# Merge and router of a mixer-and-experts block as one stage, bias parts made in the first stage, tokens turned ahead of the norm

## The reference, cut to what matters

```python
# merge_branches
ya = (rms_norm(from_heads(o_a), gdn_norm_g) * silu(za)) @ w_out_a
yb = (rms_norm(from_heads(o_b), gla_norm_g) * silu(rb)) @ w_out_b
gates = sigmoid(parts[11])
y = (gates[..., :D_MODEL] * ya + gates[..., D_MODEL:] * yb) @ w_out
# first_block
x = x + g1 * y
h = rms_norm(x, norm_ffn_g) * (1.0 + sc2) + sh2
x = x + g2 * moe_ffn(h, ...)
# moe_ffn
logits = h @ w_router + b_router
top_logit, top_idx = lax.top_k(logits, TOP_K)
top_p = softmax(top_logit)
gu = xb @ w_gu[e] + b_gu[e]
glu, lin = minimum(gu[:, :D_EXPERT], 7.0), clip(gu[:, D_EXPERT:], -7.0, 7.0)
act = glu * sigmoid(1.702 * glu) * (lin + 1.0)
y = (act @ w_down[e] + b_down[e]) * p
```

## Time and profile before

| | us |
|---|---|
| median of 3 runs | 2254.32 |
| lowest and highest run | 2253.1, 2254.37 |
| the profiled execution | 2256.12 |
| its span, first to last instruction | 2254.3 |
| TensorE busy | 1987.3 |
| VectorE busy | 699.3 |
| ScalarE busy | 498.1 |
| GpSimd busy | 74.1 |

### The profile page before, as it was taken

One profiled execution on the slowest core, in us unless ns is written; L12 is line 12 of the kernel. 1 busy time (PEld: TensorE's weight loads), 2 busy tenths in 40 slices (PEclk: granted clock), 3 DMA queues, 4 the chain that ended last, 5 costly groups with the idle time before them and its releaser, 6 DMA issues. The chain is left out here.

```text
span 2254.3 us, 25572 instructions
## 1 busy us (share of the span) xinstructions
PE 1987.3 (88%) x9450; PEld 1091.9 (48%) x9452; DVE 699.3 (31%) x1516; ACT 498.1 (22%) x931; POOL 74.1 (3%) x67
## 2 busy tenths in 40 slices
PE   6999796989898469999999999999999697879997
PEld 3346455968786233333333333333333245547774
DVE  1475363447201522221222122212222303332323
ACT  2221721453301011111111111111111203410111
POOL 0000500100000300000000000000000000000000
PEclk8999997989999679999999999999999899889998
DMA  9452346134632469999999999999999334024342
GB/s 330 148 205 90 130 108 137 53 119 129 218 134 85 163 257 417 417 417 418 417 417 418 418 418 417 417 417 418 417 418 418 121 119 162 1 89 165 140 167 84
DMA packets 149817, 565.51 MB, mean 251 GB/s; under 512 B 35840, under 2 KB 43008, under 8 KB 111904
## 3 DMA queue, kind: packets, MB, share of 16 engines
q1 hardware_dynamic: 149760, 564.73, 64.7%
HBM read 554.67 MB, written 10.03 MB: 250 GB/s over the span
## 5 line engine op out<-in xcount | busy, mean ns | idle before, releaser
L1996 PE MATMUL expert_gb<-expert_ring,hT 128*64 128x512 f32 x1024 | 262.6, 592 | 0.0
L1996 PE MATMUL expert_lb<-expert_ring,hT 128*64 128x512 f32 x1024 | 262.5, 592 | 0.0
L2028 PE MATMUL expert_yb<-expert_ring,hT 128*64 128x512 f32 x1024 | 226.8, 595 | 11.2 <-ACT hT L1951 11.2
L1904 DVE TENSOR_SCALAR hT<-expert_gb 128x512 f32<-128x512 f32 x32 | 22.1, 692 | 551.3 <-PE expert_lb L1996 551.3
L1966 PE MATMUL expert_ob<-hT,ob 128*128 128x512 f32 x256 | 125.6, 618 | 36.8 <-DVE oa L1917 24.5
L2608 PE MATMUL ffn_pu<-ffn_hT,ffn_wu 128*128 128x256 f32 x704 | 155.7, 380 | 0.0
L2608 PEld LDWEIGHTS ffn_pu<-ffn_hT,ffn_wu 128*128 128x128 f32 x704 | 134.1, 191 | 27.2 <-issue 9.6
L440 PE MATMUL mix_in_pj<-hT,mix_in_pj_ring 128*128 128x512 f32 (+1 forms) x384 | 144.3, 535 | 1.4 <-DVE hT L551 1.4
L1996 PEld LDWEIGHTS expert_lb<-expert_ring,hT 128*64 128x64 f32 x1024 | 72.3, 137 | 147.5 <-issue 147.5
L2028 PEld LDWEIGHTS expert_yb<-expert_ring,hT 128*64 128x64 f32 x1024 | 70.6, 137 | 148.7 <-issue 128.0
L1917 DVE TENSOR_TENSOR oa<-oa,expert_ob 128x512 f32<-128x512 f32 x128 | 86.4, 685 | 174.6 <-PE expert_ob L1966 174.6
(11 more groups left out here) (466 smaller groups left out, 2398.4 us busy)
## 6 DMA issues: line engine op xcount, KB each, us to landing
expert_ring<-in_w_gu SPq DMA_DIRECT2D x256, 1024.0 KB, 11.9
expert_ring<-in_w_down SPq DMA_DIRECT2D x128, 1024.0 KB, 10.1
fill_w<-in_w_fill SPq DMA_DIRECT2D x48, 512.0 KB, 3.6
mix_in_wm<-in_w_mod SPq DMA_DIRECT2D x11, 2048.0 KB, 9.6
ffn_wu<-in_w_up_units SPq DMA_DIRECT2D x22, 1024.0 KB, 5.9
mix_in_pj_ring<-in_w_in_units SPq DMA_DIRECT2D x12, 1024.0 KB, 4.8
ffn_wd<-in_w_down SPq DMA_DIRECT2D x22, 512.0 KB, 3.4
attend_in_wi<-in_w_in SPq DMA_DIRECT2D x4, 2048.0 KB, 10.8
```

The lines of the kernel that those rows point to most:

```text
L1904: v.tensor_scalar(glu, gb[:], LIMIT, None, ALU.min).then_inc(s_glu, 1)
L1996: m = pe.matmul(b[halves[h], :], xT[:, k, x], ring[:, z, c0 + 512 * h:c0 + 512 * h + 512], start=False, stop=(k == GU - 1))
L2028: m = pe.matmul(yb[halves[h], :], hidT[:, c, hh * SLOTS:(hh + 1) * SLOTS], ring[:, z, a * F + 512 * h:a * F + 512 * h + 512], start=False, ...
```

## The change

- `merge_stage` and `router_stage` become one stage, `merge_route_stage`, without the barrier between them. The stage's large tiles (`pz`, the two branch weights) lie in the expert ring; SP loads the ring's units as these tiles come free: 8 to 11 after the second branch product, 0 to 3 after `y`, 4 to 7 after the last product with `w_out`.
- The bias parts are made in `mix_in_stage` by GpSimd from biases laid out over 128 partitions (768 columns each), stored to DRAM at the end of that stage, and loaded as `bparts` in the merge.
- `x` is transposed before the norm. The router weights are multiplied by `a2`; a row of `b2` times the router weights (the shift, eight matmuls ahead of the later fill units) is added to the router bias; the logits are multiplied by the root of each token. `h2T` is copied by VectorE and ScalarE, in halves. The table of the square root and that of exp are loaded ahead. `xn`, which the experts gather, is made after the mask.
- The one-hot comparisons of all ranks and halves become one operation of 256 elements and a sum; the weights are a product with it and a second sum.
- The memsets of `wgt`, `mask`, `pos`, `posp`, `put` and `acc` are made by GpSimd in the merge.

```diff
@@ mix_in_stage, sync, after gate_cols
+                sp.dma_start(bias[:], A.bias_blocks).then_inc(s_bi, 16)
                 later(4)
@@ mix_in_stage, sync, end
-                sp.wait_ge(s_o, 96)
+                sp.wait_ge(s_bs, 7)
+                sp.dma_start(A.bias_split.rearrange("n p c -> p n c"), parts[:]).then_inc(s_o, 16)
+                sp.wait_ge(s_o, 112)
@@ mix_in_stage
+            @block.gpsimd
+            def _(g):
+                link = Chain(g, s_bs)
+                g.wait_ge(s_bi, 16)
+                for n in range(3):
+                    link(g.tensor_copy(parts[:, n, :], bias[:]))
+                    if n < 2:
+                        link(g.tensor_copy(back[:], parts[:, n, :]))
+                        link(g.tensor_tensor(bias[:], bias[:], back[:], ALU.subtract))
@@ merge_route_stage, sync, after the load of x
+                sp.dma_start(wr, A.w_router.rearrange("(k p) n -> p k n", p=P)).then_inc(s_rw, 16)
...
+                for n in range(3):
+                    sp.dma_start(S.bparts[n * NE:(n + 1) * NE].rearrange("e (b c) -> e b c", b=4),
+                                 A.bias_split[n].rearrange("(b e) c -> e b c", b=4)).then_inc(s_tab, 16)
                 for f in range(F0 + 8, F1):
                     S.fill.load(sp, f)
                 sp.wait_ge(s_pa, 1)
...
+                sp.wait_ge(S.fill.done, F1)
+                sp.dma_start(S.pick, A.bias_pick).then_inc(s_tab, 16)
+                sp.wait_ge(s_pa, 2)
+                for n in range(8, 12):
+                    load_expert_unit(sp, A, S, 0, n)
+                sp.wait_ge(s_y, 1)
+                for n in range(4):
+                    load_expert_unit(sp, A, S, 0, n)
+                sp.wait_ge(s_t, 4)
+                for n in range(4, 8):
+                    load_expert_unit(sp, A, S, 0, n)
+                sp.wait_ge(s_tab, 128)
@@ gpsimd
                 g.tensor_tensor(sq[:], S.oa[:], S.oa[:], ALU.mult).then_inc(s_sq, 1)
+                for b in (S.wgt, S.mask, S.pos, S.posp):
+                    g.memset(b[:], 0.0).then_inc(s_m, 1)
+                g.wait_ge(s_pa, 2)
+                g.memset(S.put[:], 0.0)
+                g.memset(S.acc, 0.0)
@@ scalar
+                act.activation(warm[:], C.eps[:], ACT.Sqrt)
                 for t in range(2):
                     act.wait_ge(s_z, t + 1)
-                    act.activation(junk[:], S.x[:, t, :], ACT.Square, accum_out=ss[:, t:t + 1]).then_inc(s_xs, 1)
-                    act.wait_ge(s_xs, t + 1)
-                act.wait_ge(s_n, 2)
-                act.activation(rstd[:], ss[:], ACT.Sqrt).then_inc(s_n, 1)
+                    act.activation(junk, S.x[:, t, :], ACT.Square, accum_out=ss[:, t:t + 1]).then_inc(s_xs, 1)
+                    act.wait_ge(s_n, 2 * t + 2)
+                    act.activation(rstd[:, t:t + 1], ss[:, t:t + 1], ACT.Sqrt).then_inc(s_rs, 1)
+                for t in range(2):
+                    act.wait_ge(s_tr, t + 1)
+                    act.activation(S.h2T[:, 4:8, t * P:(t + 1) * P], bank[5 + 2 * t][:].rearrange("p a n -> p (a n)")
+                                   .rearrange("p (k n) -> p k n", k=4), ACT.Copy).then_inc(s_xta, 1)
+                act.activation(warm[:], C.eps[:], ACT.Exp)
@@ tensor, before the second branch product
+                        pe.wait_ge(s_rt, 2)
+                        pe.wait_ge(s_wa, 1)
+                        for k in range(KT):
+                            m = pe.matmul(shift, C.ones, wrb[:, k, :], start=(k == 0), stop=(k == KT - 1))
+                        m.then_inc(s_rb, 1)
                         for f in range(F0 + 6, F1):
                             fill(f)
                         pe.wait_ge(S.fill.copied, F1)
+                        pe.wait_ge(s_br, 1)
@@ tensor, after the products with w_out
                 for t in range(2):
-                    pe.wait_ge(s_h, 1 + t)
+                    pe.wait_ge(s_z, 1 + t)
                     for k in range(KT):
                         b = 4 + 2 * t + k // 4
-                        m = pe.transpose(flat(b)[...], S.xn[:, t, k * P:(k + 1) * P], C.ident)
+                        m = pe.transpose(flat(b)[...], S.x[:, t, k * P:(k + 1) * P], C.ident)
                     m.then_inc(s_tr, 1)
+                for t in range(2):
+                    pe.wait_ge(s_xt, t + 1)
+                    pe.wait_ge(s_xta, t + 1)
+                    for k in range(KT):
+                        m = pe.matmul(pl[:, t, :], S.h2T[:, k, t * P:(t + 1) * P], wr[:, k, :],
+                                      start=(k == 0), stop=(k == KT - 1))
+                m.then_inc(s_l, 1)
+                pe.wait_ge(s_r, 7)
@@ vector, between the gating of the branches
+                v.wait_ge(s_rw, 32)
+                v.tensor_tensor(wrb, wr, deep(S.b2[:], NE), ALU.mult).then_inc(s_wa, 1)
...
+                v.tensor_tensor(wr, wr, deep(S.a2[:], NE), ALU.mult).then_inc(s_wa, 1)
+                v.wait_ge(s_rb, 1)
+                v.tensor_tensor(br[:], shift, br[:], ALU.add).then_inc(s_br, 1)
@@ vector, after y
+                update(0)
+                spread_of(0)
+                update(1)
                 for t in range(2):
                     v.wait_ge(s_tr, t + 1)
+                    v.tensor_copy(S.h2T[:, 0:4, t * P:(t + 1) * P], bank[4 + 2 * t][...]).then_inc(s_xt, 1)
+                spread_of(1)
...
+                for t in range(2):
+                    m = v.scalar_tensor_tensor(lg[:, t, :], pl[:, t, :], rstd[:, t:t + 1], br[:], ALU.mult, ALU.add)
+                route(m)
...
+                route(v.tensor_tensor(one[:], iota[...].to_broadcast([P, 2, TOPK, NE]),
+                                      idf[...].to_broadcast([P, 2, TOPK, NE]), ALU.is_equal))
+                route(v.tensor_reduce(S.mask[:, :, 0:NE], one[:].rearrange("p t r n -> p t n r"), AX, ALU.add))
+                for t in range(2):
+                    v.tensor_scalar(S.xn[:, t, :], S.x[:, t, :], rstd[:, t:t + 1], None, ALU.mult)
+                v.wait_ge(s_e, 1)
+                route(v.reciprocal(tot[:], tot[:]))
+                route(v.tensor_tensor(ex[:], ex[:], deep(tot[:], TOPK), ALU.mult))
+                route(v.tensor_tensor(one[:], one[:], ex[...].to_broadcast([P, 2, TOPK, NE]), ALU.mult))
+                route(v.tensor_reduce(S.wgt[:, :, 0:NE], one[:].rearrange("p t r n -> p t n r"), AX, ALU.add))
+                v.wait_ge(s_p, 1)
```

More of the change, by code:

```diff
@@ L193, in mix_in_stage @@
         ends = s.sb("ends", [32, 2, NTILE])
+        bias, back, parts = s.sb("bias", [P, 768]), s.sb("bias_back", [P, 768]), s.sb("bias_parts", [P, 3, 768], BF16)
         quant = s.sb("quant", [P, 2, 2 * L])
@@ new lines, in merge_route_stage @@
+        spare = S.fill.o[:].rearrange("p a n -> p (a n)")
+        wr = spare[:, 0:KT * NE].rearrange("p (k n) -> p k n", k=KT)
+        wrb = spare[:, KT * NE:2 * KT * NE].rearrange("p (k n) -> p k n", k=KT)
+        tri = spare[:, 2 * KT * NE:2 * KT * NE + P]
+        br, iota = s.sb("br", [P, NE]), s.sb("iota", [P, NE])
+        lg, top, idx = s.sb("lg", [P, 2, NE]), s.sb("top", [P, 2, 8]), s.sb("idx", [P, 2, 8], U32)
+        idf = s.sb("idf", [P, 2, 8])
+        ex, tot, nmax = s.sb("ex", [P, 2, TOPK]), s.sb("tot", [P, 2]), s.sb("nmax", [P, 2])
@@ new lines, in merge_route_stage @@
+        one = s.sb("one", [P, 2, TOPK, NE])
+        most = s.sb("most", [P, 1])
+        bank = [s.ps(f"bank{b}", [P, 2, L]) for b in range(8)]
+        (s_in, s_pz, s_wo, s_x, s_sq, s_ss, s_v, s_rt, s_sil, s_ya, s_pa, s_t, s_y, s_z, s_xs, s_n, s_rs, s_tr, s_xt, s_xta, s_ln, s_sqb) = (
+            s.sem(n) for n in ("in", "branch_gates_in", "wo_in", "x_in", "squared", "sums", "chain", "rooted", "silu", "gated",
+                               "branch", "mixed", "y_done", "out_done", "x_squares", "norm", "rstd_done", "turned",
+                               "x_copied", "x_copied_high", "logs_done", "linear_squared"))
@@ L1499, in merge_stage @@
+        s_rw, s_tab, s_wa, s_rb, s_br, s_l, s_e, s_p, s_r, s_m = (s.sem(n) for n in (
+            "router_w_in", "tables_in", "router_w_scaled", "shift_done", "shift_added", "logits", "exped", "placed", "route", "mask_done"))
         F0, F1 = FILL_AT["merge"]
         fbank = lambda f: bank[6 + f % 2][:].rearrange("p a n -> p (a n)")
+        pl, shift = bank[0][:, :, 0:NE], bank[5][:, 0, 0:NE]
+        pp = bank[1][:].rearrange("p a n -> p (a n)")[:, 0:3 * NE].rearrange("p (a n) -> p a n", a=3)
@@ L1634, in _, with update @@
                 v.wait_ge(s_x, 16)
-                for t in range(2):
+                def update(t):
                     for h in range(2):
```

187 lines of the change are left out of this document (60 added, 127 removed).

## The result

The changed kernel took **2226.53 us** (median of 4 runs, 2222.51 to 2228.69), the kernel before 2254.35 in the same job (median of 4, one of which took 4918.06 us and is not in the ratio): ratio 0.9876, interval 0.9857 to 0.9896. The prediction was 2224.5, range 2215 to 2235. The profiled execution took 2228.69 us, its span is 2226.9, the mean granted clock 0.951.

A forecast was written before the change was run, and what follows sets the result against it. TensorE paces merge and experts; between them VectorE's bias split and chain end last, and a shift there reaches the end whole. -38.5 + 1.9 + 0.6 + 3.7 + 2.5 = -29.8 us gives 2224.5 us, range 2215 to 2235.

The forecast's parts named there:

- The stage: Router stretch behind the last w_out product: its end moves from 804.1 to 765.6 us, a gain of 38.5 us.
- the logits: Router logits on TensorE: 32 records, seven fast and 25 slow, 6.3 us, ending at 759.1.
- the chain: VectorE's operations from the logits to the count in the router stretch: 6.3 us.
- The clock: TensorE's clock in the router stretch: expected to fall about when the logits start.
- The shift: Eight matmuls on TensorE ahead of a fill in the merge: +1.9 us (1.8 to 3.5 by the clock).
- The memsets beside y: GpSimd's memsets beside VectorE's last operations before w_out: +0.6 us, bounds 0 and 3.6.
- The store: Bias parts stored at the end of mix_in, all engines waiting at the barrier: +3.7 us (1.5 to 6).
- GpSimd beside hT: GpSimd's seven bias operations in mix_in beside VectorE's making of hT: +2.5 us, the middle of 0 and 5.
- Rival 2: Little is paid: logits at the higher clock, VectorE unblocked, memsets free, store 1.5 us; 2216.3 us, chance 0.12.
- rival 1: Ports and store at their upper ends: GpSimd blocks mix_in and y, logits slow; 2233.1 us, chance 0.20.
- The other two: Router chain still meets a late table, 2254 us, chance 0.02; experts need a second pass, 3188 us, chance 0.02.
- The pairs of experts: Expert stage: pairs still 60.2 us apart; the prediction would be wrong if they grew longer.

The follow-up runs named there:

- before_no_split: Kernel before with only the first of each bias's three bf16 parts made, the two lower set to zero: 2243.25 us, ratio 0.9933.
- before_wide_mask: Kernel before with the sixteen pairs of small mask operations replaced by one wide comparison, one product and two reductions: 2248.25 us, ratio 0.9963.
- store_early: Changed kernel with the store of the bias parts issued near 70 us, not at the end of mix_in: 2222.15 us, ratio 0.9858.
- pool_late: Changed kernel with GpSimd waiting for VectorE's sixteen hT operations before it splits the biases: 2224.44 us, ratio 0.9854.

## Why the prediction was right, point by point

- **The stage, -38.5 forecast.** Up to the count it gave (804.08 + 9.90) - 774.55 = 39.4; 0.9 more, 0.4 of it in the logits (5.88 against 6.3) and 0.3 in the chain (6.04 against 6.3). The clock fell where the prediction put it, with some luck: in the other executions with the transposes ahead of the norm and no added matmuls the logits took 5.69 to 6.88 us. before_no_split gives 14.7 of it, before_wide_mask 8.0 to 8.6, the way from the last update to the logits' sum another 14.5 (24.2 in before_no_split, 9.7 after; of it 0.6 by the turned order). That is 37 to 38. Another 1.2 are the small memsets and the copy that VectorE no longer makes (10.2 less 3.0 of waiting for GpSimd in before_wide_mask, 6.04 after), and the four make the 38.7 by which e fell: the parts hide nothing of each other. No run takes the 14.5 apart, among the barrier, the loads, the folded modulation and the tables loaded ahead; in the kernel before, 4.8 of it lay between the finished `h2T` and the logits (760.86 to 765.66).
- **The shift, +1.9 forecast.** 1.87 us of records, 1.7 to the next fill. It can't be told apart in the sum: distance d has a mean of 167.4 in the nine kernels with it and 166.3 in the three without, but one of the nine lies at 170.4.
- **The memsets beside y, +0.6 forecast: 0.** The two operations ran 2.49 and 2.29 us beside 3.6 us of memset, and w_out started 5.1 us behind the branch product as before (727.68; the earlier trace rows has 5.07). What the Trainium skill says ("SBUF — State Buffer", section "Who interferes with whom") of a GpSimd instruction that only writes, that it does not contend with a VectorE instruction with two SBUF inputs, would have been the better price; it was named and not taken. That sentence is not about the cast of 16 elements, a single-source operation, which took 1.44 and 3.18 us beside the same memsets and 0.17 alone. The same section of the Trainium skill names casts and `tensor_scalar` among the operations that can contend with GpSimd; the traces agree for both, here and in `hT`.
- **The store, +3.7 forecast.** 3.6 in the first profile, 4.1 by the means of b. The reason holds (a landing at a barrier, something given back by delta_scan's loads).
- **GpSimd beside hT, +2.5 forecast.** 2.3 in the first profile, 3.4 by the means of a, with 2.4 to 5.1 as single values. The middle between 0 and 5 was too low by 0.9, and it was a middle only, without a reason for it. The rows fit the upper end's mechanism: at 40.44 about 8 of the 16 operations were done, and the other 8 ended only at 49.37, just behind the last of GpSimd's seven (48.32 + 0.91), as if each let one pass. Why TensorE lost 2.4 us of it in one execution and 5.1 in another no run tells. The prediction says that no row shows such a meeting, but the trace of the kernel before has one, in the split of the router stage. The same cast of VectorE took 1.22 us in the first round and 3.25 in the second, where it ended 1.08 us behind the difference of GpSimd that was running:

```profile
767.30 1.22 DVE L1687 CAST bias_parts<-router_bias 32x2048 bf16<-32x2048 f32 x1 [6.44 <-DMA router_bias<-in_b_gu]
771.47 4.26 POOL L1690 TENSOR_TENSOR router_bias<-router_bias,router_back 32x1024 f32<-32x1024 f32 x1
773.56 3.25 DVE L1687 CAST bias_parts<-router_bias 32x2048 bf16<-32x2048 f32 x1
```

That row spoke for the upper end.
- **Missing: the clock behind the stage.** The prediction left 12.6 us from the count to the first expert matmul and nothing more. It was 13.35 (the gather took 6.73 instead of 5.53), and the first weights at the lower clock took 1.4 more: 2.1 us. It is not shown to be a price of the shorter stage: with the same stage store_early and pool_late have a gather of 5.30 and 5.75 us and an f of 1437.5 and 1437.9, nearly that of the kernel before, while before_wide_mask, with a stage only 8 us shorter, has 6.70 and 1439.1. It goes with when the clock comes back: in the last two-us row of the gather in the changed kernel (0.80 and, in its second profile, 0.82), one row earlier in store_early and pool_late (0.60 and 0.57). And in the first profile 3.6 us arose in unchanged stages, which the second profile of the same kernel doesn't have.

With the means the sum is -39.4 + 1.7 + 0 + 4.1 + 3.4 + 2.1 = -28.1; the medians of the two jobs are 27.8 and 29.1 below those of the kernel before. That the total came so near -29.8 is partly luck: the stage, the shift and the memsets were 1.7 us better than forecast, the store, `hT` and the clock 3.4 worse. Rival 2 (little is paid) was wrong on the store, the clock and `hT`; rival 1 had the right direction for `hT`. The other two did not occur: no table came late (the nearest, the bias row, held VectorE until 639.84, and its result was needed at 656.78), and one pass was made. The pairs of experts stayed 60.2 us apart.

## What to carry to other kernels

Work moved from a wait into "idle" places has a price in each of them: look whether the engine next to it runs back-to-back short operations from SBUF, and whether the transfer that follows is the last thing before a barrier. Here moving one store and adding one wait were worth 8 us by the distances, beside the 27.8 that were won. And where TensorE pauses in a stage, price the matmuls in and behind the pauses at the lower clock too, or fill the pauses with products that nobody reads, which gave 5 to 7 us here.

## What was not expected of the hardware

- Beside GpSimd's chain a chain of `tensor_scalar` on SBUF operands ends about when that one does (0.7 us ahead to 1.1 behind in the five kernels): 5.26 us became 11.74 in the kernel as changed, 11.10 to 11.76 in the others with the chain there.
- A cast of 128x16 elements took 3.18 us where it met two memsets, 1.44 where it met one (and the 128x2 operation next to it 1.73, for the other), 0.17 to 0.18 alone, while a sum of two 128x2048 operands (2.29 us) beside one of them lost nothing.
- A load of the router's bias row, broadcast to 128 partitions, held SP's queue for 4.41 us (up to 4.59 in the others). The same load took 0.58 in the router stage of the kernel before, so it is not the load alone; what else no run tells.
- Stretches without any edit differ by up to 4.4 us between executions (distance c), and the two longest had fills at the lower clock; one profile of each kernel would have put 3.6 us of it down to the change.
